# Two RMS norms applied inside the transposes, chunk by chunk, in a fused two-block kernel

## What is computed

```python
def rms_norm(x, g):
    y = x * rsqrt(mean(x * x, axis=-1, keepdims=True) + EPS)
    return y * g

h = rms_norm(x, attn_norm_g)                 # norm n1
proj = h @ w_in                              # glu, q, k, v, qi, ki, wi, gates
...                                          # attention with 64 selected keys, conv branch
x = x + mixed @ w_out
h2 = rms_norm(x, ffn_norm_g)                 # norm n2
q = h2 @ w_peer_q                            # queries, 2048 columns
...                                          # scores, top 16 of 16384 experts per head
act = gelu(einsum('tnd,td->tn', expert_u[e], h2)) * gate
x = x + einsum('tn,tnd->td', act, expert_v[e])
```

## Time and profile before

| what | value |
|---|---|
| median of 3 runs | 1580.61 us |
| lowest and highest | 1575.66 and 1583.27 us |
| the profiled execution's own time | 1575.73 us |
| its span in the profile | 1573.9 us |
| mean granted clock of TensorE | 0.865 |
| busy, share of the span | PE 77%, DVE 59%, ACT 27%, POOL 22% |
| chain that ended last | PE 52%, DMA 26%, DVE 11%, ACT 5% |
| read from HBM | 405.89 MB |

### The profile page before, as it was taken

The page is one execution under the profiler, slowest core; times in us unless marked ns, Lnnn a source line. Parts: engine busy times, 40 slices in busy tenths (PEclk is TensorE's granted clock), DMA queues, the critical chain, the costliest instruction groups (busy, mean ns, idle before and its releaser), DMA issues.

```text
span 1573.9 us, 26601 instructions
## 1 busy us (share of the span) xinstructions
PE 1214.3 (77%) x11250; PEld 829.7 (53%) x11250; DVE 926.6 (59%) x2059; ACT 430.3 (27%) x1087; POOL 341.1 (22%) x315
## 2 busy tenths in 40 slices
PE   7988898893475633447756775799988888999998
PEld 5567784780143200115423452357887774888843
DVE  2887665557887988796677665321355433455512
ACT  3111310132422422463354332422343211101100
POOL 1000011114453544544545454000000000000000
PEclk9997999895588755569967895899999999999999
DMA  9552459699999999999999999624300032454442
GB/s 370 183 185 71 155 186 361 240 319 416 421 418 416 415 420 420 418 411 418 418 420 420 420 419 409 263 80 161 107 9 4 4 110 84 145 161 143 141 146 105
DMA packets 109720, 409.73 MB, mean 260 GB/s; under 512 B 8456, under 2 KB 33552, under 8 KB 76448
## 3 DMA queue, kind: packets, MB, share of 16 engines
q0 software_dynamic: 44576, 297.35, 46.3%
q1 hardware_dynamic: 63552, 106.48, 19.6%
q10 hardware_dynamic: 1472, 4.20, 1.0%
HBM read 405.89 MB, written 2.11 MB: 259 GB/s over the span
## 4 chain that ended last, share of the span: by engine, by line
PE 52%; DMA 26%; DVE 11%; ACT 5%; issue 3%; POOL 2%; POOLq 0%; DVEq 0%; ACTq 0%
DMA arena<-in_experts,arena 24%; PE psum L502 22%; PE psum L512 6%; PE psum L1893 5%; PE psum L2373 5%; DVE arena L1438 4%; PE psum L1469 3%; POOL arena L1423 2%; DMA weights<-in_w_in 1%; PE psum L748 1%; PE psum L734 1%; PE psum L745 1%; PE psum L753 1%; ACT arena L1449 1%; PE psum L868 1%
## 5 line engine op out<-in xcount | busy, mean ns | idle before, releaser
L1469 PE MATMUL psum<-arena 128*32 128x512 f32 x1024 | 193.8, 840 | 262.8 <-ACT arena L1454 262.8
L1423 POOL DMA_INDIRECT arena<-in_experts,arena x256 | 311.1, 1215 | 381.9 <-PE psum L1469 304.3
L502 PE MATMUL psum<-actT,weights 128*128 128x256 f32 x1696 | 375.0, 384 | 2.9 <-DMA weights<-in_w_in 1.1
L502 PEld LDWEIGHTS psum<-actT,weights 128*128 128x128 f32 x1696 | 325.6, 192 | 51.0 <-ACT actT L624 2.6
L1469 PEld LDWEIGHTS psum<-arena 128*32 128x32 f32 x1024 | 23.1, 124 | 365.5 <-ACT arena L1454 354.8
L1438 DVE CUSTOM_DVE_ANT_0 arena<-arena 128x1024 f32<-128x1024 f32 x96 | 116.6, 1223 | 58.5 <-DMA arena<-in_experts,arena 57.9
L1438 DVE CUSTOM_DVE_ANT_0 arena<-weights,arena 128x1024 f32<-128x1024 f32 x96 | 117.2, 1225 | 56.1 <-DMA arena<-in_experts,arena 54.1
L1444 ACT ACTIVATE arena<-arena 128x2 f32<-128x2 f32 x128 | 26.0, 203 | 380.0 <-DVE arena L1438 379.9
L1893 PE MATMUL psum<-arena 64*64 64x64 f32 (+1 forms) x2816 | 82.2, 227 | 14.4 <-DVE arena L2010 7.1
L1893 PEld LDWEIGHTS psum<-arena 64*64 64x64 f32 x2816 | 78.4, 139 | 22.4 <-issue 10.8
L1438 DVE CUSTOM_DVE_ANT_0 arena<-normed,arena 128x1024 f32<-128x1024 f32 x64 | 77.1, 1224 | 21.3 <-DMA arena<-in_experts,arena 20.1
(11 more groups left out here) (392 smaller groups left out, 1683.4 us busy)
## 6 DMA issues: line engine op xcount, KB each, us to landing
weights<-in_w_in SPq DMA_DIRECT2D x18, 2048.0 KB, 8.7
arena<-in_ada_wT POOLq DMA_DIRECT2D x48, 512.0 KB, 5.8
weights<-in_ffn_w_up SPq DMA_DIRECT2D x22, 1024.0 KB, 6.5
weights<-in_ffn_w_down SPq DMA_DIRECT2D x5, 2048.0 KB, 7.8
weights<-in_w_out SPq DMA_DIRECT2D x4, 2048.0 KB, 12.7
weights<-in_w_peer_q SPq DMA_DIRECT2D x4, 2048.0 KB, 11.1
arena<-in_experts,arena POOLq DMA_INDIRECT x256, 13.3
weights<-in_w_ple_gate SPq DMA_DIRECT2D x2, 2048.0 KB, 11.0
```

Of the source, the lines that this page charges most:

```text
L502: mm = nc.tensor.matmul(out[:, c * T:(c + 1) * T], w[:, k, c * P:(c + 1) * P], act[:, k, :], start=(k == 0), stop=(k == kc - 1))
L1423: nc.gpsimd.indirect_dma_start(out=rows[:, n % RING, :], out_offset=None, in_=dram["experts"], in_offset=bass.IndirectOffsetOnAxis(ap=eidx ...
L1469: mm = nc.tensor.matmul(SUMS[sum_part(k, i), i, :], diag[:, pos, :], rows[:, pos, D + 512 * i:D + 512 * (i + 1)], start=first, stop=last, ...
```

## The change

Norms n1 and n2 take the form of the later ones. Line numbers of the changed kernel are larger by up to 19; the text uses those of the kernel before unless it says otherwise.

- n1: ScalarE loads the table for the root first (act_function), squares block 0, copies the bias table, and takes the two roots; VectorE squares block 1 and builds the diagonals. TensorE transposes xres itself, chunk by chunk, within tile glu_g. No normalised rows are written. The load of cc, which lands in normed, waits for the eight chunks instead of for the transposes, and TensorE's wait for const_rest stands behind glu_g.
- mix_out1 gives a semaphore after its first 128 tokens, so that the addition to xres and the squares of block 0 can be made while block 1 is multiplied.
- n2: the same within tile peer_q0, with the gain (now also in the small constants, ffn_g) applied while copying. VectorE writes the rows of normed with the gain only behind its chunk copies, ScalarE sends them to DRAM after that.

```diff
-        HALF_TILES = ("ple_gate1", "rw_out1")
+        HALF_TILES = ("mix_out1", "ple_gate1", "rw_out1")
...
-        ROOT_COLS = dict(n3=16, n4=32, n5=40, n6=48)
-        ROOT_STEPS = dict(act=dict(n3=("s00", "s10", "e", "root0", "root1"),
+        ROOT_COLS = dict(n1=0, n2=8, n3=16, n4=32, n5=40, n6=48)
+        ROOT_STEPS = dict(act=dict(n1=("s00", "root0", "root1"),
+                                   n2=("s00", "s10", "e", "s01", "root0", "root1"),
...
+                          dve=dict(n1=("s10", "rec0", "diag0", "rec1", "diag1"),
+                                   n2=("add0", "s11", "rec0", "diag0", "rec1", "diag1", "row0", "row1"),
...
         def pe_project(pe):
...
-            pe_turn(pe, "n1", normed, aux, ready=[("rel_cp", 1)])
-            turned(pe, "n1")
+            pe.wait_ge(S("rel_cp"), 1)
+            pe_norm_tile(pe, "n1", "glu_g")
             pe.wait_ge(S("const_rest"), 16)
-            pe_features(pe, "glu_g", actT)
             pe_features(pe, "glu_a", actT)
...
         def act_first(act):
             act.wait_ge(S("const_in"), 16)
-            act_norm(act, "n1", xres, normed, 0, ready=[("x_in", 16)])
-            act.wait_ge(S("small_in"), 16)
+            act_function("n1", ACT.Sqrt)
+            act.wait_ge(S("x_in"), 16)
+            act_squares(act, "n1", 0, junk=silu_0)
             act.wait_ge(S("rel_pe"), 1)
             nc.scalar.copy(hbias, AUX[0:AH, 0, 0:3 * P]).then_inc(S("rel_cp"), 1)
-            copy_turned(act, "n1", aux, lambda c: C("attn_g", c), None, actT, 0)
+            act_root(act, "n1", 0, whole_sum=True)
+            act_root(act, "n1", 1, whole_sum=True)
+            act.wait_ge(S("small_in"), 16)
+            copy_chunks(act, "n1", lambda c: C("attn_g", c), None, 0)
...
         def dve_first(dve, st):
...
-            dve_norm(dve, st, "n1", xres, normed, 0, ready=[("x_in", 16)])
+            dve.wait_ge(S("x_in"), 16)
+            dve_squares(dve, "n1", normed[:, 0, :], None)
+            dve.wait_ge(S("const_in"), 16)
+            dve_diagonals(dve, "n1")
             dve.wait_ge(S("small_in"), 16)
-            copy_turned(dve, "n1", aux, lambda c: C("attn_g", c), None, actT, 1)
+            copy_chunks(dve, "n1", lambda c: C("attn_g", c), None, 1)
...
         def add_product(dve, name, tag):
-            for i in range(2):
-                dst = xres[:, :, 512 * i:512 * (i + 1)]
-                nc.vector.tensor_tensor(dst, toks(product(dve, f"{name}{i}")), dst, ALU.add).then_inc(
-                    freed(f"{name}{i}"), 1)
+            dst = xres[:, :, 0:512]
+            nc.vector.tensor_tensor(dst, toks(product(dve, f"{name}0")), dst, ALU.add).then_inc(freed(f"{name}0"), 1)
+            for b in range(TB):
+                dst = halves_of(xres, b, 1)
+                nc.vector.tensor_tensor(dst, toks(half_product(dve, f"{name}1", b))[:, b, :], dst, ALU.add).then_inc(
+                    freed(f"{name}1") if b else S("norm_dve"), 1)
...
-            pool.wait_ge(S("turn_pe"), so_far("n1", DC // 2, DC // 2))
+            pool.wait_ge(S("chunk_pe"), DC)
...
         def pe_queries(pe):
-            pe_turn(pe, "n2", normed, aux)
-            turned(pe, "n2")
+            pe_norm_tile(pe, "n2", "peer_q0")
...
-                if i < QUARTERS:
+                if 0 < i < QUARTERS:
                     pe_features(pe, f"peer_q{i}", actT)
...
         def act_queries(act):
+            act_function("n2", ACT.Sqrt)
             wait_freed(act, "mix_out0")
-            act_norm(act, "n2", xres, normed, 8, ready=[(f"freed{tile_at['mix_out1'] % 2}", tile_at["mix_out1"] // 2 + 1)], gain=True)
-            copy_turned(act, "n2", aux, None, None, actT, 0)
-            act.wait_ge(S("normed_ok"), so_far("n2", TB, TB))
+            for b in range(TB):
+                act_squares(act, "n2", b, 0)
+            act_first_half(act, "n2")
+            act.wait_ge(S("norm_dve"), norm_at("dve", "n2", "add0"))
+            act_squares(act, "n2", 0, 1)
+            act_root(act, "n2", 0)
+            act_root(act, "n2", 1)
+            copy_chunks(act, "n2", lambda c: C("ffn_g", c), None, 0)
+            act.wait_ge(S("norm_dve"), norm_at("dve", "n2", "row1"))
             act.dma_start(normed_rows.rearrange("(b p) d -> p b d", p=P), normed).then_inc(S("normed_out"), 16)
...
         def dve_queries(dve, st, mod):
...
+            dve_squares(dve, "n2", normed_flat[:, 0:512])
+            dve_diagonals(dve, "n2")
+            copy_chunks(dve, "n2", lambda c: C("ffn_g", c), None, 1)
             dve.wait_ge(S("gbc_in"), 16)
-            dve_norm(dve, st, "n2", xres, normed, 8, gain=gbc)
-            copy_turned_plain(dve, "n2")
+            dve.wait_ge(S("chunk_pe"), chunks_before("n2") + DC)
+            for b in range(TB):
+                nc.vector.scalar_tensor_tensor(normed[:, b, :], xres[:, b, :], root_of("n2", b), gbc,
+                                               ALU.mult, ALU.mult).then_inc(S("norm_dve"), 1)
             for _ in mod:
                 pass
```

31 lines of the change are left out of this document (15 added, 16 removed).

## The result

| what | before | after |
|---|---|---|
| median of six runs | 1579.68 us | 1570.68 us |
| lowest and highest | 1575.66 and 1583.27 us | 1567.2 and 1574.97 us |
| the profiled execution's own time | 1575.73 us | 1574.97 us |
| its span | 1573.9 us | 1573.2 us |
| ratio of the times, with its 95% interval | | 0.9948 (0.9927 to 0.997) |

Three more runs of the kernel before were made beside those of the changed one. The change makes the kernel faster by 0.52%, some 8 to 9 us: more than the 0.5% that such a measurement can tell from no change, as forecast, and the forecast time of 1570.5 us is met within 0.2 us.

A forecast was written before the change was run, and what follows sets the result against it. The prediction took TensorE to bound mostly the first 340 us and full-rate DMA the gathers after. Gains of 3.0 us (n1) and 7.1 us (n2) made 10.1 us, 1570.5 us against the median of 1580.61, range 1563 to 1579.

The forecast's parts named there:

- The bound: Up to the choice of experts: time taken from the chain ahead of the first gather starts all gathers equally earlier.
- the gathers' length: Expert gathers, 345 to 1000 us: fixed bytes at full DMA rate, so their length was to stay unchanged.
- n1: 3.0 us forecast: First norm, within glu_g: TensorE starts at 9.8 us, the tile ends at 29.4 instead of 32.35 us, 3.0 us gained.
- the prediction's reason: At n1: if diagonal products counted no more than transposes for the clock, 20.5 us would stay, the sum 0.9 us less.
- n2: 7.1 us forecast: Second norm, from mix_out1 to the choice: peer_q0 ends 7.2 us sooner, of which 7.1 us reach the choice.
- the modulation: VectorE behind n2: twelve rows at 1.75 us take 21.0 us, ready at 310.3 against scores at 310.4, just covered.
- rival A: Modulation behind n2 takes the cover and more: peer_q2's 2 MB add 5.0 us, 1573.3 us in all; chance 0.16.
- the store of the rows of normed: Behind n2: the rows reach DRAM 4 us later, are read only behind the first scores, and cost nothing.
- The sum: Both norms together: 3.0 + 7.1 = 10.1 us, giving 1570.5 us against the median; chance 0.56.
- B: Start bound elsewhere, by tile q's landing or glu_g's half clock: the first norm gives nothing, 1573.5 us; chance 0.12.
- C: Gathers begin earlier but work woven between them sets their end: half the gain lost, 5 us, 1575.6 us; chance 0.10.
- D: ScalarE's wait for all 48 modulation rows decides: 3.8 us per waited-for row, slower, 1584.6 us; chance 0.06.

The follow-up runs named there:

- n2_only: Kernel before with only the second norm and the halves of mix_out1 in the new form, n1 as before: 1571.21 us, ratio to before 0.9966.
- before_again: The kernel before, not edited, run once more for a second profile: 1577.75 us.
- before_plus5: Kernel before with four unused VectorE instructions, 5.0 us, between n2's copies and the modulation: 1579.52 us, ratio to before 1.0008.
- whole_add: Changed kernel with mix_out1 again given over whole and added to xres in one piece: 1571.48 us, ratio to before 0.9969.
- n1_only: Kernel before with only the first norm in the new form, n2 and mix_out1 as before: 1576.2 us, ratio to before 0.9993.
- after_again: The changed kernel, not edited, run again beside others on one chip: 1570.78 us, ratio to before 0.9952.
- keep_clock5: Changed kernel with five unread products of constants in TensorE's pause ahead of mix_out0: 1567.98 us, ratio to before 0.9926.
- rows_late: Changed kernel with four modulation rows put ahead of n2's two rows of normed on VectorE: 1571.79 us, ratio to before 0.9973.
- after_plus5: Changed kernel with n2's rows of normed written three times, 5.0 us more on VectorE ahead of the modulation: 1578.34 us, ratio to before 1.0008.
- keep_clock: Changed kernel with ten unread products of constants in TensorE's pause ahead of mix_out0: 1570.96 us, ratio to before 0.9958.
- combined: Changed kernel with five unread products ahead of mix_out0 and five modulation rows moved beside mix_out1: 1569.76 us, ratio to before 0.9938.

## Why the prediction was right

**The bound.** It was right to follow the chain only up to the choice. 7.1 us sooner at the choice is 7.1 us sooner at the first gather, 327.37 against 334.46. That the gathers' length would be left alone was not exact: on average 668.9 us with either part of the change and 672.0 without. The difference has arisen by the 65th of the 256 gathers, which starts 167.5 to 169.4 us behind the first instead of 170.7 to 171.7. What causes it is not settled; no run was made for it alone.

**n1: 3.0 us forecast, 3.2 between the two profiles, 1.8 on average** at the end of glu_g. The start was 0.3 us later than forecast (10.1 for 9.8), the tile 0.6 shorter (19.0 for n4's 19.57). For the new form the forecast was good beyond this pair: in the ten profiles with the new n1 it takes 19.0 to 20.4 us from the first product to the end of glu_g, 19.6 on average. The mis-sized term is the old form, whose 20.5 us were read from one execution. It took 20.5 and 20.7 us in before and n2_only but 18.6 in before_again and in before_plus5, on average 19.6 as well. So the tile gave nothing, the earlier start 1.8 us, and that 3.0 were met by the first pair was luck. The chain of before_again, against the earlier trace rows:

```profile
16.41 14.07 PE psum L502 x64
...
30.50 15.32 DMA weights<-in_w_in
```

and its timeline on TensorE at the start of tile q:

```profile
45.86 14.43 PE L512 MATMUL psum<-weights,actT 128*128 128x512 f32 x33 [1.58 <-DMA weights<-in_w_in]
```

Its glu_g ends 1.9 us before that of the kernel before, but tile q is not there yet when glu_a ends, and TensorE starts it only 0.4 us sooner. In the kernels with the new n1 tile q came in time, so what counts, the start of tile q, is 2.5 us sooner on average (43.5 for 46.0).

In the new form the first twelve records took 2.90 us, the time of half the clock (whole_add's took 2.93 at 0.50 and after's in n2 1.83 at 1.00), although the column of the granted clock shows 1.00 there; from 14 us on they run at the full pace in the kernel after. On the page "TensorE: Matmul & The Clock Gate" of the Trainium skill, Part 4 says that plain transposes do not count as activity in the way products do. The runs agree with it in some places and not in others. In the kernel before, n2's sixteen transposes left the clock at half for 3 us more, and so it was in before_again and before_plus5; but in n1_only it came back by 281 us, when TensorE had done nothing but sixteen transposes since its pause, and in before_again and before_plus5 the 64 records of glu_g, right behind n1's sixteen transposes, took 14.07 us, where glu_a's 64 take 13.81 at the full pace. So the rule is not shown. Products by a diagonal brought no shorter tile on average, but not for the prediction's reason either: the old form, too, was often faster than its 20.5 us.

Part of n1's gain is spent again at mix_out0, where TensorE waits longer and more often at its lower clock: in the averages of the profiles 4.4 us at the end of att_out1 are 3.3 at the end of mix_out1. Why it is 4.4 there and 2.5 at tile q is open, and the spread within the groups is as large. The time of n1_only shows 1.1 us, with an interval from 3.3 faster to 1.1 slower.

**n2: 7.1 us forecast, 6.2 seen.** The restart was forecast 1.9 us behind mix_out1 and came at 1.99; peer_q0 was forecast at +19.9 and ended at +19.9, in seven of the nine kernels with the halves to a hundredth (19.90 or 19.91), the two others being those whose clock fell behind n2's pause. The table load left the path. The mis-sized term is the modulation: twelve rows at 1.75 us were to take 21.0 us; they took 22.4 in after and 22.5 in after_again, 1.9 each, and 23.2 or 23.3 in keep_clock5 and n2_only. The choice came at +36.4 and not at +35.4. Loads of modulation rows, kernel after, 280 to 311 us (the kernel before had 3.7/5.2/5.7 in its stretch):

```profile
DMA to landing us min/median/max: 5.2/7.0/7.9
```

This is rival A, the cover taken and more, at about a third of its size: 1.0 us and not the 2.8 that all of peer_q2's bytes among the rows would cost. "DMA: Bandwidth & Descriptors" in the Trainium skill, section on queues, rings and completion order, has each DMA engine take turns between its queues; the slower landings beside peer_q2's load agree with that, and with a plain shortage of bandwidth as well. Nor is peer_q2 the whole of it. Its load is asked for at 294.00 us, and the fifth row, which started at 294.09, had by then waited 2.13 us where it waited 0.62 in the kernel before. What ran beside the first loads is the store of the rows of normed, 1024 KB, asked for at 287.42, 1.4 us ahead of the first of these loads; in the kernel before it was 3.0 us ahead. The first load took 5.2 us to land against 3.7, and in rows_late, where that store comes 5.6 us behind the first load, it took 3.9. So the store, whose move the prediction put at nothing, has a share of the missing microsecond; how much was not tried by a run of its own. The row that the term was read from, 1.75 us beside mix_out0's loads, had such an overlap, but with mix_out1's load under way from before; here the load is asked for in the middle of the rows.

**The sum.** 3.0 + 7.1 = 10.1 us against 8.2 to 9.0 measured. By averages of the profiles: 3.3 at mix_out1, 6.2 more up to the choice (of after) and 3.1 in the gathers come to 12.6, less 4.2 behind the gathers: 8.4. So the number was met with two effects that were not forecast and nearly cancel. The prediction was right on the chain round n2, met n1's size by the luck of one pair of profiles, and was lucky behind the choice.

**The rivals.** A was in part true. B did not happen: in the kernels with the new n1, glu_a and tile q each started when the tile ahead of it ended. In before_again and before_plus5, of the old form, TensorE did wait for tile q, for 1.6 and 1.1 us. C, the gathers giving half back, was wrong in sign; it is the stretch behind them that gives back. D, the slower case, did not happen: the waited-for rows took 1.9 us each and not 3.8. after_plus5 shows how near its side is: 5 us more on VectorE undo the whole change.

**The 4 us behind the gathers**, an average of 352.5 less one of 348.3, go with a lower clock of TensorE over some 350 us: 0.96 or 0.97, and 0.97 or 0.98 in the three profiles without the change. The stretches lie elsewhere from one profile to the next (1190 to 1230 and 1260 to 1290 us in the one of after). That the profiles with the change are all longer here, by 0.2 to 9 us, is measured; why an earlier start should do it is open. Three profiles stand on one side only.

## What to carry to other kernels

A step that moves work off the waiting engine's path puts it on another's: add up that engine's rows up to the same consumer, loads included, and if the margin comes out at nothing, take from it what else has to be done there first (five rows moved into an idle time gave back the whole margin at the choice). A term read from a row of the same form elsewhere in the trace was good to some tenths of a microsecond for instructions and to 7 to 11% for a string of loads: a load asked for in the middle of the string is not the same as one already running. A stretch of the kernel before, too, is one draw: n1's took 20.5 us in one execution and 18.6 in another, and the gain forecast from it was too large by as much as it varies. Judge a change of half a per cent by medians of several runs and each part at its own place; the spans of one pair of profiles hid the whole gain.

## What the runs showed of the hardware

- **A pause of TensorE can cost more than its length.** Ahead of mix_out0, pauses of 3.3 to 3.9 us left the granted clock at 1.00 in three profiles and took it to half in one (before_again, 3.57 us); the seven of 3.97 us and more, up to 5.3, all took it to half, and the tiles then took 1.7 to 2.1 us longer. In n2 a pause of 2.0 us left it at 1.00 in seven kernels and took it to half in keep_clock and combined, 1.7 us each time; there it fell some 1.2 us after TensorE had begun again. What else than the pause's length decides is open.
- **Filling such a pause keeps the clock there.** With five or ten products whose results nothing reads the clock stayed at 1.00 and the mix_out tiles took 27.7 us in all three kernels that have them, instead of 29.4 and more; in two of the three it fell at n2 instead. The kernel with five had the lowest time, 0.9926 (0.9904 to 0.9949) of before, but the interval overlaps that of the change without them (0.9927 to 0.997). A product of 32-bit data, 128 rows by 512 columns, takes two records of 0.43 us; too many of them delay the tile behind.
- **A load of 512 KB took 7.0 us to land (median of eight) instead of 5.2** when a store of 1024 KB ran beside the first of them and a load of 2 MB from another queue started among them, and up to 10.6 in after_plus5, where store and load both ran beside the first four.
- **Sixteen transposes can be followed by either clock.** Behind them the next tile ran at the full pace at once in three of eight places (n1 in before_again and before_plus5, n2 in n1_only), and at half the pace for its first 3 to 4 us in the other five.
